# Down projection: a set's four weight sums in one side buffer, two of them made by one operation, and the second slab split by its second block alone

## What is computed

```
def conv_ffn(h, w_up, conv_w, conv_b, w_down):
    S = h.shape[1]
    u = h @ w_up
    up = jnp.pad(u, ((0, 0), (CONV_WIDTH - 1, 0), (0, 0)))
    u = conv_b + conv_w[0] * up[:, 0:S] + conv_w[1] * up[:, 1:S + 1] + conv_w[2] * up[:, 2:S + 2]
    g, val = u[..., :D_FF], u[..., D_FF:]
    return (jax.nn.silu(g) * val).astype(h.dtype) @ w_down
```

## Time and profile before

| | us |
|---|---|
| device time, median of 3 runs | 2438.64 (2438.13 to 2439.71) |
| span of the profiled execution | 2436.8 |
| PE busy | 2420.0 (99%) |
| DVE busy | 1837.0 (75%) |
| ACT busy | 1370.6 (56%) |
| first layer's sets | 1007 to 1192 |
| second layer's sets | 2222 to 2408 |

### The profile page before, as it was taken

The page is one execution under the profiler, slowest core; times in us unless marked ns, Lnnn a source line. Parts: engine busy times, 40 slices in busy tenths (PEclk is TensorE's granted clock), DMA queues, the critical chain, the costliest instruction groups (busy, mean ns, idle before and its releaser), DMA issues.

```text
span 2436.8 us, 34545 instructions
## 1 busy us (share of the span) xinstructions
PE 2420.0 (99%) x12376; PEld 2060.6 (85%) x12376; DVE 1837.0 (75%) x2597; ACT 1370.6 (56%) x1959; POOL 57.5 (2%) x108
## 2 busy tenths in 40 slices
PE   9999999999999999999999999999999999999998
PEld 7888888888888888888788888888888888888886
DVE  7658877677777677888876588776777776778887
ACT  6545655665555555555555456566655555555554
POOL 0000000000000000000000003000000000000000
PEclk9999999999999999999999999999999999999999
DMA  8755455566656656666766665565666565656665
GB/s 299 248 186 190 155 171 174 179 207 183 199 180 193 195 181 189 206 208 210 230 199 190 200 197 174 169 184 175 208 189 200 175 196 184 192 184 209 209 217 194
DMA packets 251642, 476.87 MB, mean 196 GB/s; under 512 B 18032, under 2 KB 21248, under 8 KB 251520
## 3 DMA queue, kind: packets, MB, share of 16 engines
q1 hardware_dynamic: 234640, 447.83, 58.3%
q10 hardware_dynamic: 16880, 27.43, 3.6%
HBM read 468.89 MB, written 6.31 MB: 195 GB/s over the span
## 4 chain that ended last, share of the span: by engine, by line
PE 92%; DVE 3%; ACT 2%; DMA 2%; issue 1%; POOL 0%; ACTq 0%; POOLq 0%; DVEq 0%
PE acc L2249 15%; PE aux L2249 8%; PE acc L2257 8%; PE acc L2222 7%; PE acc L2224 7%; PE acc L2223 7%; PE tp L2249 7%; PE acc L2228 6%; PE acc L2229 6%; PE acc L2230 6%; PE aux L2257 4%; PE tp L2257 4%; DVE w_lo L1317 1%; PE tp L2228 1%; PE aux L2228 1%
## 5 line engine op out<-in xcount | busy, mean ns | idle before, releaser
L1317 DVE TENSOR_TENSOR w_lo<-raw,w_hi 128x1024 fp32r<-128x1024 f32 x847 | 1016.1, 1221 | 410.4 <-ACT w_hi L625 409.9
L625 ACT ACTIVATE w_hi<-raw 128x1024 fp32r<-128x1024 f32 x847 | 867.3, 1054 | 367.2 <-DVE raw L2049 82.7
L2249 PE MATMUL acc<-a_hl,w_hi 128*128 128x512 f32 x1568 | 486.6, 392 | 0.0
L2249 PEld LDWEIGHTS acc<-a_hl,w_hi 128*128 128x128 f32 x1568 | 281.9, 189 | 47.4 <-issue 0.2
L2257 PE MATMUL acc<-a_hl,w_lo 128*128 128x256 f32 x1568 | 315.0, 283 | 0.0
L2222 PE MATMUL acc<-w_hi,a_hl 128*128 128x512 f32 x700 | 279.0, 399 | 1.8 <-DVE a_hl L1346 1.2
L2224 PE MATMUL acc<-w_hi,a_hl 128*128 128x512 f32 x700 | 273.4, 391 | 0.0
L2223 PE MATMUL acc<-w_lo,a_hl 128*128 128x512 f32 x700 | 272.6, 389 | 0.0
L2257 PEld LDWEIGHTS acc<-a_hl,w_lo 128*128 128x128 f32 x1568 | 256.9, 191 | 15.3
L2249 PE MATMUL aux<-a_hl,w_hi 128*128 128x512 f32 x832 | 256.9, 390 | 0.0
L2249 PE MATMUL tp<-a_hl,w_hi 128*128 128x512 f32 x736 | 227.3, 390 | 0.0
(11 more groups left out here) (369 smaller groups left out, 3286.7 us busy)
## 6 DMA issues: line engine op xcount, KB each, us to landing
raw<-in_w_up SPq DMA_DIRECT2D x352, 512.0 KB, 4.4
raw<-in_w_down SPq DMA_DIRECT2D x176, 512.0 KB, 4.6
raw<-in_w_in_c SPq DMA_DIRECT2D x96, 512.0 KB, 4.4
raw<-in_w_in_ab SPq DMA_DIRECT2D x95, 512.0 KB, 4.5
raw<-in_w_out_ab SPq DMA_DIRECT2D x32, 512.0 KB, 4.6
raw<-in_w_out_c SPq DMA_DIRECT2D x32, 512.0 KB, 4.3
raw<-in_w_mk SPq DMA_DIRECT2D x16, 512.0 KB, 4.3
raw<-in_w_mq SPq DMA_DIRECT2D x16, 512.0 KB, 4.0
```

The costliest lines, as they stand in the source:

```text
L625: act.activation(w_hi[:, s], raw[:, s], ACT.Copy).then_inc(hi_ready, 1)
L1317: dve.tensor_tensor(w_lo[:, s], raw[:, s], w_hi[:, s].bitcast(F32), ALU.subtract).then_inc(lo_ready, 1)
L2249: last = pe.matmul(bank, w_hi[:, slot, j, f * P:(f + 1) * P], both, start=(kt == 0), stop=(kt == KT - 1))
```

## The change

The four sums get a buffer of four places: `t_sum`, `t_hi`, `t_lo` are 128 x 4 x 512 instead of 128 x 3 x 512, and `raw` is no longer written.

- DVE makes O0 - E0 and O1 - E1 by one operation of 128 x 1024 into `t_sum[0]` and `t_sum[1]`. Then `t_sum[2]` = O1 - `t_sum[0]`, and `t_sum[3]` = E1 - `t_sum[2]`. Each of the two waits for the one before.
- ACT and DVE split of O the second block alone (128 x 512), and ACT no longer waits for DVE before that.
- `t_hi` and `t_lo` are made in operations of 128 x 2048 instead of 128 x 1536.
- PE does for O block product 6 (3 matmuls) by `w_hi`, `w_lo`, then waits for `t_lo`, then does block products 3, 4, 2 and 5 (12 matmuls) by the sums.

```
-        t_sum = place("t_sum", [P, 3, N], at=a_at + 2 * KB)
-        t_hi = place("t_hi", [P, 3, N], F32R, at=a_at + 8 * KB)
-        t_lo = place("t_lo", [P, 3, N], F32R, at=a_at + 2 * KB)
+        t_sum = place("t_sum", [P, 4, N], at=a_at + 2 * KB)
+        t_hi = place("t_hi", [P, 4, N], F32R, at=a_at + 10 * KB)
+        t_lo = place("t_lo", [P, 4, N], F32R, at=a_at + 2 * KB)
...
+            def split_second(n, s):
+
+                act.wait_ge(raw_landed[s], landed(n, s))
+                act.wait_ge(slab_used, n - (RING - 1))
+                act.activation(w_hi[:, s, 1, :], raw[:, s, 1, :], ACT.Copy).then_inc(hi_ready, 1)
...
-                        act.wait_ge(*DV(L, "t_sum", 4 * m + 2))
-                        split(n + k, (n + k) % RING)
+                        split_second(n + k, (n + k) % RING)
                         act.wait_ge(*DV(L, "t_sum", 4 * m + 4))
                         act.activation(t_hi[:], t_sum[:], ACT.Copy).then_inc(LS(L, "t_hi"), 1)
...
+            def split_second(n, s):
+
+                dve.wait_ge(hi_ready, n + 1)
+                dve.tensor_tensor(w_lo[:, s, 1, :], raw[:, s, 1, :], w_hi[:, s, 1, :].bitcast(F32), ALU.subtract)\
+                    .then_inc(lo_ready, 1)
...
-                        dve.tensor_tensor(t_sum[:, 2, :], raw[:, s1, 1, :], raw[:, s1, 0, :], ALU.subtract).then_inc(done, 1)
-                        dve.tensor_tensor(raw[:, s1, 0, :], raw[:, s1, 0, :], raw[:, s0, 0, :], ALU.subtract)\
+                        dve.tensor_tensor(t_sum[:, 0:2, :], raw[:, s1, :, :], raw[:, s0:s1 + 1, 0, :], ALU.subtract)\
                             .then_inc(done, 1)
+                        dve.wait_ge(*DV(L, "t_sum", 4 * m + 1))
+                        dve.tensor_tensor(t_sum[:, 2, :], raw[:, s1, 1, :], t_sum[:, 0, :], ALU.subtract).then_inc(done, 1)
                         dve.wait_ge(*DV(L, "t_sum", 4 * m + 2))
-                        dve.tensor_tensor(t_sum[:, 0, :], raw[:, s1, 1, :], raw[:, s1, 0, :], ALU.subtract).then_inc(done, 1)
-                        dve.wait_ge(*DV(L, "t_sum", 4 * m + 3))
-                        dve.tensor_tensor(t_sum[:, 1, :], raw[:, s0, 1, :], t_sum[:, 0, :], ALU.subtract).then_inc(done, 1)
+                        dve.tensor_tensor(t_sum[:, 3, :], raw[:, s0, 1, :], t_sum[:, 2, :], ALU.subtract).then_inc(done, 2)
                         split(n + k, s0)
                     else:
-                        split(n + k, (n + k) % RING)
+                        split_second(n + k, (n + k) % RING)
...
-                        by_weights(tp[:, 1, :], 3, 0, first, last)
                         by_weights(acc[:, 1, 0, :], 6, 1, False, False).then_inc(slab_used, 1)
                         pe.wait_ge(*DV(L, "t_lo", m + 1))
-                        by_sums(aux[:, 0, :], 4, 0, first, last)
-                        by_sums(acc[:, 0, 1, :], 2, 1, False, False)
-                        by_sums(aux[:, 1, :], 5, 2, first, last).then_inc(LS(L, "seven_used"), 1)
+                        by_sums(tp[:, 1, :], 3, 0, first, last)
+                        by_sums(aux[:, 0, :], 4, 2, first, last)
+                        by_sums(acc[:, 0, 1, :], 2, 3, False, False)
+                        by_sums(aux[:, 1, :], 5, 1, first, last).then_inc(LS(L, "seven_used"), 1)
```

More of the change, by code:

```diff
@@ L235, in build @@
         hid_f2 = place("hid_f2", [P, FF_KT, SEQ], at=big_at + FF_KT * KB)
-        t_sum = place("t_sum", [P, 3, N], at=a_at + 2 * KB)
-        t_hi = place("t_hi", [P, 3, N], F32R, at=a_at + 8 * KB)
-        t_lo = place("t_lo", [P, 3, N], F32R, at=a_at + 2 * KB)
+        t_sum = place("t_sum", [P, 4, N], at=a_at + 2 * KB)
+        t_hi = place("t_hi", [P, 4, N], F32R, at=a_at + 10 * KB)
+        t_lo = place("t_lo", [P, 4, N], F32R, at=a_at + 2 * KB)
         st_at = [base + 3584 * q for q in range(UP_SEVENS)]
-        st_at += [a_at + 14 * KB + 3584 * q for q in range(SEVENS - UP_SEVENS)]
+        st_at += [a_at + 18 * KB + 3584 * q for q in range(SEVENS - UP_SEVENS)]
         st_hi = [place(f"st_hi_{q}", [P, 7, P], F32R, at=st_at[q]) for q in range(SEVENS)]
```

## The result

| | kernel before | changed kernel |
|---|---|---|
| device time, median of 13 runs each, us | 2439.71 (2437.92 to 2443.28) | 2445.29 (2442.11 to 2447.03) |
| span of the profiled execution | 2436.8 | 2443.7 |
| time that PE loses around the sets | 1.7 | 7.3 |

The ratio is 1.002, with a 95% interval of 1.0013 to 1.0027: the change makes the kernel slower by 0.13% to 0.27%, 3 to 7 us. The forecast was +2.7 us and a range up to 2445.0. Its direction and mechanism hold. Its size is half of what the medians show, and the median lies 0.3 us above the range's end, while the kernel before is itself 1.1 us above the median of its first three runs. By the ratio, 1.002 times 2438.64 is 2443.5. It lies on the bound of 0.2% itself, between "within" (0.83) and "slower" (0.16).

A forecast was written before the change was run, and what follows sets the result against it. PE, busy 99%, bounds the kernel, so only its stalls can change. Four stretches lose 0.7, 0.7, 0.94 and 0.95 us, 3.3 together, less 0.6 for O's earlier load: 2438.64 + 2.7 = 2441.3 us, range 2438.0 to 2445.0.

The forecast's parts named there:

- "ready" and "asked": Around each set's sums: PE asks for `t_lo` 0.68 us earlier and may load 0.26 later; 0.94 us of slack used.
- The sums: DVE's sums in each set end 2.67 us after the first sum's start instead of 2.74, 0.07 saved.
- "Nothing lost": Sets 1 to 3 come 10.20 us apart, PE's own pace, winning nothing back; sets like set 5 lose nothing.
- the quiet ones: The sixteen sets 3 to 7, 9 to 12, 21 to 23, 25 to 28, with 0.95 to 1.01 us of slack.
- the first 0.11 of a delay costs PE nothing: At PE's held loads: the next load follows in 0.11 us instead of 0.23, so delays up to 0.11 are free.
- The sets like set 5 lose nothing: In the sixteen sets with 1.00 us to spare: 0.94 used, 0.06 left and 0.11 of grace, nothing lost.
- The loads of O, 0.6 us back: Last three sets of each layer: O's load issued earlier gives 0.1 us per set, 0.6 us back in all.
- The bound of zero, 3.3 us: If O landed no earlier than before in the last three sets of a layer, the loss would be 3.3 us.
- the forecast's first count: Second halves before O's earlier load is credited: 0.94 us lost by set 15, 0.95 by set 31.
- Rival A: Last sets of each layer: O's load profits by the full 0.6 us per set; +0.5 remain, 2439.1 us; chance 15%.
- Rival B: All sets: the chain of `t_hi` and `t_lo`, 0.3 us longer, takes over; +6.0, 2444.6 us; chance 16%.
- Rival C: DVE's one operation less per set, 0.07 us, goes to PE's held loads; time 2437.3 us; chance 6%.

The follow-up runs named there:

- e4_before_late3: Kernel before with PE's three matmuls of block product 3 moved behind the wait for `t_lo`, DVE and ACT unchanged; ratio 1.0007 to the kernel before.
- e6_two_sums: Changed kernel with the joined first sum taken apart into two 512-column operations and all increments by 1; ratio 1.0012 to the kernel before.
- e2: Changed kernel with `t_hi` made in two operations, the first as soon as two sums are there; ratio 1.0006 to the kernel before.
- e3: Changed kernel with `t_hi` and `t_lo` each in two halves, PE waiting for each half of `t_lo` separately; ratio 0.9998 to the kernel before.
- e7: Changed kernel with `t_hi` and `t_lo` in halves, increment by 1, and DVE's split of E ahead of the sums; ratio 0.999 to the kernel before.
- e1: Changed kernel with the last sum adding 1 to its semaphore instead of 2, counts 3 per set; ratio 1.0014 to the kernel before.

## Why the prediction was right, and by how much it was short

- **PE loses what stands between "ready" and "asked".** Right. PE asks 0.68 us earlier (shown alone by e4_before_late3) and `t_lo` is ready later; together every set loses its slack of 1 us. In set 0 the matmuls around the held load start 1.15 us and then 0.34 us apart instead of 0.23 each: 1.03 us lost, 0.88 expected there.
- **The sums.** The first operation took 1.23 (1.22 taken). The step that failed is "a sum that waits for the one before starts 0.03 to 0.04 after its end": 0.10 in one of two places, by the increment by 2, which I had read as free. With 0.02 more in the sums it made "ready" 7.08 and not 7.00.
- **"Nothing lost" in sets 1 to 3 and in the quiet ones.** "DVE's time from set to set becomes 10.20, just PE's own" was 10.28, 0.08 too much four times in each first half, 0.3 together. The quiet sets came 10.23 to 10.25 apart in sets 9 to 12 and 21 to 23 and not 10.20; those of the last half 10.20. There PE asks at 7.06, so that the load is held by a mere 0.024, and "the first 0.11 of a delay costs PE nothing" does not hold as it stands: most of the matmuls behind it start 0.228 to 0.236 apart instead of 0.227, and each such set loses about 0.03. In the last half the load is held by 0.022 and nothing is lost. Why so little decides it is open.
- **"The sets like set 5 lose nothing" forgot the chance of a late O.** Set 6 of the changed kernel has its sums at 1070.36, 10.72 after set 5's, held by the load; set 19 likewise. In the kernel before, set 19 was late by 0.39 of waiting for a load too, and PE lost nothing. Its slack absorbed it. Now each costs 0.4. Such a late load came to one to three sets of the first halves in ten of the twelve profiled executions, in places that differ. This and the 0.08 are the larger part of what the first halves lost over the forecast (1.7 each against 0.7).
- **The loads of O, 0.6 us back.** No sign of them. The argument fits the runs (more traffic makes O later, an earlier issue moves it by nothing that can be told), and the value taken still allowed for a tenth per set. The bound of zero, 3.3 us, was nearer. With 0.08 more in each of the four places, 0.3 in each first half and the two late sets it comes to about 5.1 of the 5.6, and the quiet sets add some 0.2. What the two second halves lose, 2.2 us over the kernel before, also depends on how late O happened to be in each execution; that they come near the 1.9 of the forecast's first count is in part luck.
- **Rival A** (the loads win it back) falls by the distances above. Its sum had PE's load 0.15 late and called that "within the grace" of 0.11, 0.04 too kindly; nothing hangs on it. **Rival B** (the chain exceeds the grace in all quiet sets) did not come: 7.08 is inside 7.17; the quiet sets paid 0.03 at most (not for the reason of B, as said above) and not 0.13. **Rival C** (the saved start-up goes to PE) falls by e6_two_sums: joining gains nothing on the chain.

The rule of the Trainium skill ("Perfetto Trace Analysis", Optimizing Scalar/DVE Operations) that breaking up instructions may let work finish sooner where Scalar or Vector cause bubbles without being saturated agrees with what e2, e3 and e7 show here: `t_hi` of 1.92 us in two of 1.06 took 0.33 us off the chain.

## What to carry to other kernels

Where an engine that is 99% busy waits for a side engine, read for each such wait how long before the question the answer is ready: this slack, not the side engine's busy share, is what a change spends, and it also pays for transfers that come late by chance. A change that removes an operation and keeps the number of columns can still lose if it moves work behind the last input or the question ahead of it. Halves that follow their inputs, and work that needs no late input put ahead of the wait, gave the slack back; but the latter only where the engine has no new idle time in its own row.

## What the runs showed of the hardware

- A DVE operation with an increment of its semaphore by 2 started 0.06 us later than with one by 1 (gap of 0.10 and 0.04 behind the same operation). With the 2 its wait stood as an instruction of its own in the trace, with the 1 it did not.
- A DVE operation that waits for the one just ahead starts 0.03 to 0.05 us after its end; one that doesn't overlaps it and starts 0.61 after its start (512 columns, 0.69 long). Two single sums of which the next needs only the first were 0.05 faster for it than one joined sum.
- The three steps from set to set with parked loads beside the weights (12 to 15, 28 to 31) take 30.6 to 33.4 us in the kernel before and e1 to e4, e6, e7 and the changed one, with no trend between an issue of O's load at 5.0, 4.5 or 3.7 us after the first sum, and 36.9 to 37.1 with the added copies. What decides from execution to execution which set gets its load late is open.
